# Hyena pairs made within their stage, the last mixer's stages joined, and attention scores issued two blocks ahead

## The reference, cut to what matters

```python
# layer 0 of the second model: Hyena's way out, joined with mLSTM's cells
g = (v * x1);  y = irfft(rfft(g) * rfft(k2)) + g * bias;  hy = y * x0
y_lat = concatenate([hy_l, ml_l], -1) @ w_out      # and the same for the context
# layer 1: MLA, 8 heads, 512 queries, 768 keys (context and own tokens)
q_n, q_r = split(rmsnorm(q_a) @ w_uq)              # 128 plain and 64 turned values a head
q_r, k_r = rope(q_r), rope(k_r)                    # k_r is shared by all heads
k_n, v = split(rmsnorm(kv_a) @ w_ukv)
s = (q . k) * 192 ** -0.5;  p = softmax(s);  o = p @ v
```

## Time and profile before

| | |
|---|---|
| median of 3 executions | 3353.38 us (3352.47 to 3353.8) |
| profiled execution, its own time | 3363.05 us |
| its span, first to last instruction | 3361.3 us |
| TensorE, matmuls | 3113.8 us, 93% of the span |
| TensorE, weight loads (beside matmuls) | 2676.0 us, 80% |
| VectorE | 1886.8 us, 56% |
| ScalarE | 1113.1 us, 33% |
| GpSimd | 100.9 us, 3% |
| mean granted TensorE clock | 0.953 |

### The profile page before, as it was taken

The page is one execution under the profiler, slowest core; times in us unless marked ns, Lnnn a source line. Parts: engine busy times, 40 slices in busy tenths (PEclk is TensorE's granted clock), DMA queues, the critical chain, the costliest instruction groups (busy, mean ns, idle before and its releaser), DMA issues. The chain is left out here.

```text
span 3361.3 us, 39885 instructions
## 1 busy us (share of the span) xinstructions
PE 3113.8 (93%) x16210; PEld 2676.0 (80%) x16210; DVE 1886.8 (56%) x2813; ACT 1113.1 (33%) x1642; POOL 100.9 (3%) x78
## 2 busy tenths in 40 slices
PE   7978999999889999999877789999999769999998
PEld 5667888886678888899854389999999656599897
DVE  5745775756555878764456645534543344366464
ACT  4443422234434222433343033212222234343232
POOL 0031000000220000000000010000000000000000
PEclk9988999999989999999988789999999889999999
DMA  3100554521104555312101021121122010123222
GB/s 125 51 26 19 181 165 152 184 76 51 45 1 134 197 171 194 106 62 97 50 1 55 0 95 58 62 70 56 63 71 87 30 43 1 39 94 104 86 97 85
DMA packets 73138, 275.79 MB, mean 82 GB/s; under 512 B 7836, under 2 KB 11420, under 8 KB 71805
## 3 DMA queue, kind: packets, MB, share of 16 engines
q1 hardware_dynamic: 72956, 273.25, 24.3%
HBM read 264.83 MB, written 8.39 MB: 81 GB/s over the span
## 5 line engine op out<-in xcount | busy, mean ns | idle before, releaser
L122 PE MATMUL banks<-normed_hi,weights_hi 128*128 128x384 f32 (+2 forms) x2672 | 886.6, 338 | 6.4 <-DVE normed_lo L1023 6.4
L123 PE MATMUL banks<-normed_lo,weights_hi 128*128 128x384 f32 (+2 forms) x2672 | 884.1, 337 | 0.0
L104 ACT ACTIVATE weights_hi<-weights_raw 128x1024 fp32r<-128x1024 f32 (+3 forms) x365 | 395.9, 1085 | 1269.5 <-PE banks L125 1210.4
L125 PE MATMUL banks<-normed_hi,weights_lo 128*128 128x384 f32 (+2 forms) x2672 | 742.8, 338 | 0.0
L110 DVE TENSOR_TENSOR weights_lo<-weights_raw,weights_hi 128x1024 fp32r<-128x1024 f32 (+3 forms) x365 | 460.3, 1261 | 126.7 <-ACT weights_hi L104 122.9
L122 PEld LDWEIGHTS banks<-normed_hi,weights_hi 128*128 128x128 f32 x2672 | 503.4, 188 | 34.4 <-DVE normed_lo L1023 6.7
L123 PEld LDWEIGHTS banks<-normed_lo,weights_hi 128*128 128x128 f32 x2672 | 505.4, 189 | 27.3
L125 PEld LDWEIGHTS banks<-normed_hi,weights_lo 128*128 128x128 f32 x2672 | 472.9, 189 | 27.4
L123 PE MATMUL banks<-hidden_lo,weights_hi 128*128 128x512 f32 (+1 forms) x880 | 323.0, 367 | 0.0
L122 PE MATMUL banks<-hidden_hi,weights_hi 128*128 128x512 f32 (+1 forms) x880 | 323.0, 367 | 0.0
L125 PE MATMUL banks<-hidden_hi,weights_lo 128*128 128x512 f32 (+1 forms) x880 | 294.7, 367 | 0.0
(11 more groups left out here) (409 smaller groups left out, 4234.2 us busy)
## 6 DMA issues: line engine op xcount, KB each, us to landing
weights_raw<-in_w_up SPq DMA_DIRECT2D x176, 512.0 KB, 3.4
ada_tiles<-in_ada SPq DMA_DIRECT2D x96, 512.0 KB, 3.4
weights_raw<-in_w_down SPq DMA_DIRECT2D x64, 704.0 KB, 4.0
weights_raw<-in_w_in SPq DMA_DIRECT2D x67, 512.0 KB, 3.4
weights_raw<-in_w_out SPq DMA_DIRECT2D x32, 512.0 KB, 3.4
x_kept<-x SPq DMA_DIRECT2D x2, 3072.0 KB, 10.8
x<-x_kept SPq DMA_DIRECT2D x1, 3072.0 KB, 10.8
weights_raw<-in_mla_down SPq DMA_DIRECT2D x6, 512.0 KB, 3.4
```

Of the source, the lines that this page charges most:

```text
L104: act.activation(self.hi[:, n % 2, 0:w], self.raw[:, n % 2, 0:w], ACT.Copy).then_inc(self.high_ready, 1)
L122: pe.matmul(out, self.hi[:, s, m], xh, start=k == 0, stop=False)
L123: pe.matmul(out, self.hi[:, s, m], xl, start=False, stop=False)
L125: mm = pe.matmul(out, self.lo[:, s, m], xh, start=False, stop=k == kt - 1)
```

## The change

1. **Hyena.** `split_tiles` goes. ScalarE copies the cells (tiles 4 to 7) to `mixed_hi` behind its last copy of the Hyena stage; VectorE makes their rests between the last `multiply` and the first `leave`. `leave` writes its tile to one of two buffers (`made`); ScalarE makes `hi` of it, and VectorE the rest (`rest`) behind the next `leave`.
2. **The last mixer.** Query projection, rope, values and key projection become one Line. SyncE loads `w_v` ahead of the query projection's own tiles. ScalarE and VectorE split it within the projection (behind its steps 8 and 9). `Values` puts one `swap` product of the rope behind each of the first five value tiles, in PSUM banks 6 and 7; the value tiles use the Line's three slots. There is one buffer for the turned product instead of two.
3. **Attention.** `scores` is issued two blocks ahead instead of one. VectorE takes the maximum of block n + 1 before it waits for the exponential of block n. The fifth product takes all 128 rows of the stacked queries and of the keys' rest, instead of 64.

```diff
+        self.tiles += n
+        self.first -= n
+        return t
 
     def buffer(self, name, shape, offset, dtype=F32):
...
+            if self.also and j == 8:
+                act.wait_ge(Z.mix["values_in"], 16)
+                act.activation(self.also.high[:], self.also.w[:], ACT.Copy).then_inc(Z.mix["values_hi"], 1)
...
+                dve.tensor_tensor(self.also.low[:], self.also.w[:], self.also.high[:].bitcast(F32),
+                                  ALU.subtract).then_inc(Z.mix["values_split"], 1)
 
 
...
+class ValueWeights(Stage):
+
+
+    def __init__(self, Z, w, high, low, source):
+        self.Z, self.w, self.high, self.low, self.source = Z, w, high, low, source
+
+    def sync(self, sp):
+        sp.dma_start(self.w[:], self.source).then_inc(self.Z.mix["values_in"], 16)
...
+        return self.Z.banks[:, n:n + 2]
+
+    def tensor(self, pe):
+        Z, on, H = self.Z, self.Z.mix, self.latents
+        W = self.weights
+        pe.wait_ge(on["values_split"], 1)
+        for t in range(6):
+            Z.room(pe, self.t0 + t)
+            for n in range(2):
+                for k in range(2):
+                    for m, (h, w) in enumerate(((0, W.high), (0, W.low), (1, W.high))):
+                        mm = pe.matmul(self.product(t)[:, n], H[h][:, 3 + k, t * P:(t + 1) * P],
+                                       w[:, k, n * 512:(n + 1) * 512], start=k == 0 and m == 0,
+                                       stop=k == 1 and m == 2)
+            mm.then_inc(on["values_ready"], 1)
+            if t < 5:
+                if t:
+                    pe.wait_ge(Z.evacuated, self.queries_at + t)
+                if t >= 2:
+                    pe.wait_ge(on["rope_turned"], t - 1)
+                pe.matmul(Z.spread_ps[:, t % 2], Z.K["swap"], self.tiles[t], start=True,
+                          stop=True).then_inc(on["rope_swapped"], 1)
+
+    def scalar(self, act):
+        on, W = self.Z.mix, self.weights
+
+        def high(n):
+            act.wait_ge(on["rope_turned"], n + 1)
+            if n == 0:
+                last = act.activation(self.keys_hi, self.keys, ACT.Copy)
+            else:
+                for m, r in enumerate(self.ROWS):
+                    last = act.activation(self.stacked[r, 2 * n - 2 + m], self.queries[r, n - 1], ACT.Copy)
+            last.then_inc(on["rope_hi"], 1)
+        act.wait_ge(self.Z.evacuated, self.t0)
+        for t in range(6):
+            act.wait_ge(on["values_ready"], t + 1)
+            act.activation(self.out[:, t].rearrange("p (n w) -> p n w", n=2), self.product(t),
+                           ACT.Copy).then_inc(self.Z.evacuated, 1)
+            if t:
+                high(t - 1)
+
+    def vector(self, dve):
+        Z, on = self.Z, self.Z.mix
+        chain = Chain(dve, on["rope_step"])
+
+        def low(n):
+            dve.wait_ge(on["rope_hi"], n + 1)
+            if n == 0:
+                dve.tensor_tensor(self.keys_lo, self.keys, self.keys_hi.bitcast(F32),
+                                  ALU.subtract).then_inc(on["rope_lo"], 1)
+                return
+            for m, r in enumerate(self.ROWS):
+                last = dve.tensor_tensor(self.stacked[self.ROWS[1 - m], 2 * n - 2 + m], self.queries[r, n - 1],
+                                         self.stacked[r, 2 * n - 2 + m].bitcast(F32), ALU.subtract)
+            last.then_inc(on["rope_lo"], 1)
...
+        for n, x in enumerate(self.tiles):
+            dve.wait_ge(on["rope_swapped"], n + 1)
+            if n:
+                dve.wait_ge(on["rope_turned"], n)
+            chain.step(dve.tensor_tensor(self.turned, Z.spread_ps[:, n % 2], Z.K["rope_sin"], ALU.mult))
+            chain.step(dve.tensor_tensor(x, x, Z.K["rope_cos"], ALU.mult))
+            dve.tensor_tensor(x, x, self.turned, ALU.add).then_inc(on["rope_turned"], 1)
+            if n:
+                low(n - 1)
+        low(4)
 
 
...
@@ -1342,9 +1399,10 @@
                                        start=t == 0, stop=t == kt - 1)
                     mm.then_inc(mixed_ready, 1)
                 scores(0)
+                scores(1)
                 for n in range(NQ):
-                    if n + 1 < NQ:
-                        scores(n + 1)
+                    if n + 2 < NQ:
+                        scores(n + 2)
                     turn(n)
                     if n % 4 == 0 and n:
                         mix(n // 4 - 1)
...
                 chain = Chain(dve, dve_step)
-                for n in range(NQ):
+
+                def top(n):
                     dve.wait_ge(scores_ready, n + 1)
                     if n >= 2:
                         dve.wait_ge(exp_done, n - 1)
@@ -1368,6 +1427,11 @@
                     src = ps[:, n % 2, 0, 0:512] if nb == 1 else ps[:, n % 2, :, 0:384]
                     chain.step(dve.tensor_reduce(s[:, 0:1], src, AX.X if nb == 1 else AX.XY, ALU.max))
                     dve.tensor_scalar(s[:, 1:2], s[:, 0:1], -scale, None, ALU.mult).then_inc(max_ready, 1)
+                top(0)
+                for n in range(NQ):
+                    if n + 1 < NQ:
+                        top(n + 1)
+                    s = sm[:, n % 2]
                     dve.wait_ge(exp_done, n + 1)
                     chain.step(dve.reciprocal(s[:, 3:4], s[:, 2:3]))
...
+        made = [spare[:, (4 + n) * SEQ:(5 + n) * SEQ] for n in range(2)]
...
+            LEAVES = [(seg, m) for seg in (1, 0) for m in range(4)]
...
+                for m in range(4, 8):
+                    act.activation(high[:, m], mixed[:, m], ACT.Copy).then_inc(left_hi, 1)
+                for n, (seg, m) in enumerate(LEAVES):
+                    act.wait_ge(left, n + 1)
+                    act.activation(by_parity(high[:, m], seg), parts(made[n % 2], seg), ACT.Copy).then_inc(left_hi, 1)
...
-                    dve.tensor_tensor(by_parity(mixed[:, m]), out, by_parity(hy[:, m]), ALU.mult)
+                def leave(n, y):
+                    seg, m = LEAVES[n]
+                    out = parts(o[:, n % 2], seg)
+                    chain.step(dve.scalar_tensor_tensor(out, by_parity(hy[:, 8 + m], seg), c("hy_bias")[:, m:m + 1],
+                                                        parts(y, seg), ALU.mult, ALU.add))
+                    if n >= 2:
+                        dve.wait_ge(left_lo, 4 + n - 1)
+                    dve.tensor_tensor(parts(made[n % 2], seg), out, by_parity(hy[:, m], seg),
+                                      ALU.mult).then_inc(left, 1)
+
+                def rest(n):
+                    seg, m = LEAVES[n]
+                    dve.wait_ge(left_hi, 4 + n + 1)
+                    dve.tensor_tensor(by_parity(low[0][:, m], seg), parts(made[n % 2], seg),
+                                      by_parity(high[:, m], seg).bitcast(F32), ALU.subtract).then_inc(left_lo, 1)
                 dve.tensor_tensor(hy[:, 8:12], hy[:, 8:12], hy[:, 4:8], ALU.mult).then_inc(gated, 1)
...
-                    leave(1, m, pt[:, m // 2, m % 2], m)
-                dve.wait_ge(y_ready, 5)
-                for m in range(4):
-                    leave(0, m, pt[:, 2, m // 2, (m % 2) * CTX:(m % 2 + 1) * CTX], m)
+                    dve.wait_ge(left_hi, m + 1)
+                    dve.tensor_tensor(low[1][:, m], mixed[:, 4 + m], high[:, 4 + m].bitcast(F32),
+                                      ALU.subtract).then_inc(left_lo, 1)
+                for n, (seg, m) in enumerate(LEAVES):
+                    dve.wait_ge(y_ready, n + 1 if seg else 5)
+                    leave(n, pt[:, m // 2, m % 2] if seg else pt[:, 2, m // 2, (m % 2) * CTX:(m % 2 + 1) * CTX])
+                    if n:
+                        rest(n - 1)
+                rest(len(LEAVES) - 1)
...
+        Z = Line(nc, K, R, 0, mix=Values.COUNTS)
+        own, both = form_of(lseg), form_of(SEGS)
+        weights = ValueWeights(Z, W, Wh, Wl, dram["mla_uv"])
+        uq = Plain(Z, 12, own.operand(H, first=CTX), own, lambda j: Hm[0][:, j], lambda j: Hm[1][:, j], qr, 8,
+                   also=weights)
+        values = Values(Z, weights, H, vt, qr, kr[:], qs, krh[:], krl[:], turned[:], 8)
+        Z.run(weights, uq, values, Plain(Z, 8, both.operand(H, 3), both, kh, lambda j: kl[:, j]))
...
-            r = slice(64 * (h % 2), 64 * (h % 2) + 64)
             qh, ql = (x[:, h, q0:q0 + P] for x in Hm)
             return [(qh, kh(h)), (qh, kl[:, h]), (ql, kh(h)), (qs[:, h, q0:q0 + P], krh),
-                    (qs[r, h, q0:q0 + P], krl[r])]
+                    (qs[:, h, q0:q0 + P], krl)]
...
+                nc.alloc_sbuf_tensor_at(unique(name), [P, n, TOK], F32R, offset=spots.base + at * TOK * ROW)
+                for name, n, at in (("mixed_hi", KT, 12), ("mixed_lo", 4, 20), ("cells_lo", 4, 4)))
+            hyena(nc, K, c, hy, ins, X, mixed_hi, (mixed_lo, cells_lo))
+
+        def mixed_pairs(k):
+            low = mixed_lo[:, k] if k < 4 else cells_lo[:, k - 4]
+            return [(mixed_hi[:, k, a:a + w], low[:, a:a + w]) for a, w in form_of(SEGS).cuts]
```

(31 more changed lines are left out.)

70 lines of the change are left out of this document (18 added, 52 removed).

## The result

The changed kernel takes 3293.43 us (median of 4 executions, 3292.25 to 3303.92); beside it on the same chip the kernel before took 3352.93 (4 executions, 3352.19 to 3353.8). The ratio is 0.9829, 95% interval 0.9809 to 0.985: 59.5 us less, where 56.6 was forecast and 3297 predicted. Taken again later it stood at 3293.16 (ratio 0.9816, 0.9799 to 0.9833).

A forecast was written before the change was run, and what follows sets the result against it. TensorE's matmuls, filling 93% of the span, were taken to bound the kernel. Terms of -6 (Hyena), -29 (last mixer) and -21.6 (attention) sum to -56.6; off the median of 3353.4 that gives 3297 us, range 3284 to 3312.

The forecast's parts named there:

- A: Hyena stage, rests made in pairs by ScalarE and VectorE instead of GpSimd: 6 us less, bounds -7 and 0.
- The price of a rest: Hyena: a whole-tile subtraction on VectorE costs 0.96, not the 2.31 seen beside GpSimd.
- B: Last mixer, stages joined into one Line: 29 us less, bounds -32 and -22.
- The load's: Query projection: the first query tile lands behind the 1 MB `w_v`, costing +0.9 once, bounds 0 and 2.
- The third key tile's wait: Key projection: VectorE enters it behind, so TensorE waits for the tile's weights, +1.0.
- The slow starts: Last mixer: stages behind a pause run partly at TensorE's lower clock; losing this saves 3.4.
- C: Attention, full-row fifth product and scores two ahead with the maximum first: 21.6 us less, bounds -25 and -12.
- the bound of -25: Attention: the most gain allowed, if the low clock at the start (0.72 over 18 us) ends earlier.
- (2): Attention: width is free, gaps belong to the operand change; only 1 to 2 us gained there, 3317; chance 0.06.
- (3): Attention: VectorE's loop binds, as hand-overs cost 0.2 more than counted; 10 us back, 3307; chance 0.07.
- (4): Last mixer: joined Line paced by VectorE or the query tiles' loads; gains only 20, total 3306; chance 0.07.
- (5): Attention: denser scores make the granted clock fall, slower than before; 3402 at 1.2 GHz; chance 0.02.

The follow-up runs named there:

- the part alone: Kernel before plus one part of the change: joined Line only, 3325.95 us (ratio 0.9913); attention only, 3328.54 us (ratio 0.9919).
- the later load: Changed kernel with `w_v` issued behind the query projection's first two loads instead of ahead of them: 3293.4 us, ratio 0.982 against the kernel before.

## Why the prediction was right, by its own steps

**A, forecast -6.** 7.0 in both traces. The price of a rest was right: 0.89 in a row, as 0.96 less 0.1 of overlap, and far from 2.31. The sentence on the Trainium skill (SBUF — State Buffer, on the shared port pair) said that the low price holds by that page; the trace agrees, with GpSimd idle here. Hyena ends 16.5 behind `multiply` instead of 11.9, 4.7 later where 5.8 was worked out. The overlap is what was taken, near 0.1 an instruction (starts 0.60 apart for rests of 0.69). Missing from the sum was a second wait that the rests fill, the 0.52 ahead of the fourth gate; a rest of 512 columns took 0.69 and not the gate's 0.75; and the last tile's copy cost a wait of 0.16 where 0.4 was taken.

**B, forecast -29.** 27.4 in the traces, 29.5 by the median of the part alone. Two terms are off. The load's was taken at +0.9; the wait is 1.65 here and up to 2.0 in other profiles, and with the later load the first scores came 2.0 sooner. I counted the first query tile as landing behind `w_v`; but `w_v` took 6.0 from its issue instead of 4.8. The other the sum lacked: TensorE's pause between the key projection and attention is 5.38 and not 4.11. ScalarE waits 0.95 for a weight tile of the next stage (the row of `in_w_out`), so VectorE's last rest ends 4.1 behind TensorE's last key matmul instead of 3.2, and the scores come behind that. The joined Line alone doesn't do this: the pause is 4.26 in that kernel, 5.50 in the one with the Hyena pairs alone, and 5.3 to 6.1 in all six that have the pairs, against 4.1 to 4.3 in the five that don't. Why the pairs, made far earlier in the program, move it isn't shown. The third key tile's wait is 1.06 (forecast 1.0), with two more near 0.2. `w_v_lo` ended 0.35 ahead of the first value matmul, about as close as forecast. The value tiles are even, as counted: a `swap` every 3.63 (forecast 3.6), without a wait. The slow starts are gone: the granted clock is 1.00 from 2684.4 to 2706.0, where it was 0.89 and 0.93.

**C, forecast -21.6.** 26.7 in the traces, 26.9 by the median of the part alone, beyond the bound of -25 that I had given. The mechanism was as put: full rows end the gaps, and VectorE's loop doesn't bind once the maximum comes first. Two terms were mis-sized, the start more than the rest. Seven steady heads give 7 x (17.84 - 14.73) = 21.8, forecast 7 x 2.9 = 20.3: a block is 2.40 and not 2.47, since the six transposes cost 0.58 here (2803.70 to 2804.28) and not 0.63. The rest of the 26.7, 4.9, is the start, for which the forecast left 21.6 - 20.3 = 1.3: the first `mix` starts 18.0 after the first scores instead of 22.8. Only 4.2 of the first stretch of attention are at the lower level and not 10.2, and half of those 6 is 3; the bound of -25 had named it. But the same start stood at 21.0 and 21.9 in the two other kernels with this attention, so one to two of the 4.9 are the spread of one profile.

The Trainium skill (TensorE: Matmul & The Clock Gate, LDWEIGHTS) speaks of a load whose time doesn't depend on the rows. By it widening gains nothing; the kernel with full rows only gained 12.05 and its gaps were gone, so for a 64-row product among 128-row ones the measurement decides otherwise. That was the right side to take, from 0.37 against 0.18.

**The rivals.** (2) falls by the full rows alone. (3) doesn't happen in the changed kernel (TensorE's blocks at 2.40), but stands where the early maximum is taken out, at 2.93 a block. (4) only as the 1.65 above. (5) didn't happen, but the kernel with scores one ahead shows the clock falling inside attention: with a pause of about 2 in each block it is granted at 0.83, and attention takes 220.3. The changed kernel has the same products without that pause and is granted 1.00 from 2734.1 to 2846.7; so it is the loop that pauses, and not dense scores, that has the low clock.

**The baseline.** Taking the sum off the median and not off the profiled execution was right: of the 69.3 between the spans, some 8 are of that one execution of before. The other 61 are 7.0, 27.4 and 26.7, where 56.6 was forecast. That 3293.43 lies within 4 of 3297 is more exact than its parts: B came out 1.6 short and A and C 6.1 over, against one profile of either kernel, and the medians gave 59.5 at first and 62.0 later.

## What to carry to other kernels

Where two engines' rounds are equally long, price each edit with the other's round held: the order alone gave 1.5, the cheaper product alone 12.05, both 26.9, and the early maximum without scores made ahead was slower than no change. Look at the starts of neighbouring matmuls for one with fewer rows: it cost 0.27 and 0.37 around it where full rows cost 0.18, and padding it with rows that are there anyway was free. Joining stages pays the barriers, the loads and the slow starts at once; the price here was what a big load did to the small ones behind it in the queue, under 2 us.

## What the hardware showed that I had not expected

**The low stretch at the start of attention was mostly shorter with full rows.** Windows over the first 14.00 us of attention, first in the kernel before, then with the order alone, then with full rows alone (the last but two figure is the granted clock):

```profile
2772.37:2786.37 14.00, 14.00 (x46) 9.85 (x46) 4.91 (x10) 4.11 (x8) 0.00 (x0) 0.63 0.00 0
```
```profile
2765.30:2779.30 14.00, 13.99 (x37) 9.54 (x38) 4.24 (x10) 3.23 (x5) 0.00 (x0) 0.53 0.00 0
```
```profile
2762.58:2776.58 14.00, 12.53 (x66) 11.57 (x67) 6.52 (x14) 6.73 (x14) 0.00 (x0) 0.88 0.00 0
```

All come behind a pause of 4 to 6 us, these three behind 4.1 to 4.2. The four profiles with 64-row products have 0.53 to 0.79 here, the seven with full rows 0.78 to 0.88. The two groups touch, one profile of each kernel stands behind them, and the cause isn't shown: a tendency, no more.

**The same code at either level in two executions.** VectorE's timeline of the Hyena filters, which wait for TensorE's products, in the kernel before and in the changed one:

```profile
1856.06 1.23 DVE L2835 TENSOR_TENSOR filters<-hyena_ps,filter_decay 128x1024 f32<-128x1024 f32 x1 [2.12 <-PE hyena_ps L2703]
1859.47 1.23 DVE L2835 TENSOR_TENSOR filters<-hyena_ps,filter_decay 128x1024 f32<-128x1024 f32 x1 [2.19 <-PE hyena_ps L2703]
```
```profile
1857.34 1.22 DVE L2915 TENSOR_TENSOR filters<-hyena_ps,filter_decay 128x1024 f32<-128x1024 f32 x1 [0.42 <-PE hyena_ps L2769]
1859.06 1.22 DVE L2915 TENSOR_TENSOR filters<-hyena_ps,filter_decay 128x1024 f32<-128x1024 f32 x1 [0.49 <-PE hyena_ps L2769]
```

3.41 a filter against 1.72, with six of them: some 8 us. The granted clock from 1852 to 1867 is 0.50 in the first and 1.00 in the second. All ten other profiles, also of kernels that are the same as before up to this place, have the 1.7. A profiled execution can be off by that much in a stretch that nobody touched.
